# Eight weight pieces of the next group split during the output's passes, and x's eight tiles ahead of the context's eight

## The chip, the cores and the metric

The kernel runs on one core of one Trainium2 chip. The metric is the device time of the whole program in microseconds (us), and the median of several runs is what counts. The core has five engines, each with an instruction queue of its own: TensorE (PE in the rows; PEld is its weight load), VectorE (DVE), ScalarE (ACT), GpSimd (POOL) and SyncE (SP), which here only issues DMAs. They meet at semaphores. An instruction that waits holds up all that stands behind it on its own engine.

## What is computed

Two layers of a transformer over 256 latent tokens ("x") and 256 context tokens, 1024 channels wide. Each layer has a mixer block (four kinds of attention from one projection `w_in`, gated and merged, then `w_out`) and a SwiGLU block (`w_ffn_in`, `w_ffn_out`). Around both stands a sandwich of RMS norms:

```python
def rmsnorm(x, g):
    xf = x.astype(jnp.float32)
    y = xf * lax.rsqrt(jnp.mean(xf * xf, axis=-1, keepdims=True) + EPS)
    return (y * g.astype(jnp.float32)).astype(x.dtype)

def gated_merge(gate_pre, branches, w_branch, w_out):
    o = jnp.stack(branches, axis=2)
    up = jnp.einsum('btnw,nwd->btnd', o, w_branch)
    g = jax.nn.sigmoid(gate_pre.reshape(up.shape))
    return jnp.sum(g * up, axis=2) @ w_out

def swiglu(u, w1, w2):
    a, b = jnp.split(u @ w1, 2, axis=-1)
    return (jax.nn.silu(a) * b) @ w2
```

What matters here is the seam between two blocks. The block's output y (tokens by 1024) is normed and added to the residual stream H, H is normed again into u, u is scaled and shifted by the conditioning, and the next block begins with u times its first weight matrix. The last layer's context tokens are not needed after its keys and values, so there the second half works on the 256 latent tokens alone.

## The kernel before

**Numbers.** All is float32, made of two fp32r parts: a high part (rounded by ScalarE) and a low part (the rest, by VectorE or GpSimd). A product is three matmuls: high by high, low by high, high by low.

**Weights.** A weight piece is 128 rows by up to 512 columns. SyncE loads it into one of four places of `load_ring` (256 KB, as two DMAs of 128 KB where its columns come from two places). A step `split` then makes its parts: ScalarE's copy makes the high part (line 1538), and then VectorE (1738) or GpSimd (1493) makes the low part, into one of the five places of `w_ring`. The load of piece i may begin when the low part of piece i-4 is made. `build_plan` writes all steps into one list in order; each engine runs its own steps in that order. At its end (1046 to 1060) a loop puts the splits in: before a step of piece n all pieces up to n+3 are split, as far as the place of `w_ring` has been given back (`piece_used`).

**The output** (`output`, 895) writes y in two halves of 512 channels. For each half it takes 8 pieces (mixer) or 22 (SwiGLU), and each piece serves all four token tiles (128 tokens each; two in the last layer's case). The last five pieces of the second half are different: `passes(tt, ...)` runs all five for token tile 0, then for tile 1, and so on, so that tile 0 is done early. So all five places of `w_ring` stay taken until the last tile's passes. While passes run, the norms of the tiles already done are made: sum of squares of y (`ysq`, ScalarE, 1555), y times the gain (`yg`, VectorE, 1820), its root (GpSimd, 1460), new H (`hn`, 1841), sum of squares of H (`hsq`, ScalarE, 1562), root, and u = H times root in two halves (`un_a`, `un_b`, VectorE, 1859).

**The next group** (`begin`, 339) is the first product of the next block: eight pieces ("first 0" to "first 7"), each of which feeds four PSUM banks at once. For each of the eight tiles of 128 channels, TensorE transposes u (`ut`, 2127), ScalarE scales and shifts it and makes the high part (`apA`, 1594 and 1599), VectorE makes the low part (`apB`, 1865), and then come the matmuls (2150 with the high part of u, 2155 with its low part). x's tokens are tiles 0 and 1, the context's are 2 and 3. The order is: x with pieces 0 to 4, the context with pieces 0 to 4 (256 columns each), then pieces 5 to 7 with all 512 columns. `hooks` puts norm steps of token tiles 2 and 3 between these. Transposed tiles go through three banks in turn (`turned_by`, 300).

There are three such seams: **seam 1**, layer 0's mixer output to its SwiGLU (about 750 to 803 us in the trace); **seam 2**, layer 0's SwiGLU output to layer 1's mixer (about 1143 to 1189 us); **seam 3**, layer 1's mixer output to its SwiGLU, x alone (about 1637 to 1671 us). At seam 3 a step `warm` runs 26 matmuls whose results are not used while the norms end.

## Time and profile before

| | us |
|---|---|
| median of 3 runs | 1860.78 |
| the three runs | 1861.15, 1853.61, 1860.78 |
| the profiled execution | 1853.27 |
| its span, first to last instruction | 1851.3 |
| TensorE busy | 1756.7 (95%) |
| VectorE, ScalarE, GpSimd busy | 1152.2, 875.3, 585.9 |
| mean granted TensorE clock | 0.983 of full |

The profiled execution lies at the lower of the three runs, and two of the three are some 7.5 us longer. A time in the rows is one of that execution, counted from the span's start. Busy time of TensorE is no measure of its speed, as its matmuls overlap: a matmul of 512 columns is shown with 390 ns, and the next begins 227 ns after it. So lengths are taken here from start to start.

### The profile page before, as it was taken

Reading aid. Unit: us, or ns where it says so; the run is one execution under the profiler, and the core shown is the slowest. Engines: PE = TensorE matmul, PEld = TensorE weight load, DVE = VectorE, ACT = ScalarE, POOL = GpSimd, SP = SyncE. Lnnn points to the kernel's source line nnn. Section 1 sums busy time; section 2 is a strip of 40 time slices with the busy share of each in tenths; the row PEclk is TensorE's granted clock in tenths of the full one; section 3 lists DMA queues with packets and bytes.
Section 4 is the critical chain, followed back from the end, with each engine's and each line's share of the span. In section 5 each row is a group of like instructions: output and inputs, shape, how many; then the busy total and the mean of one; then the engine's idle time right before and its main releaser. Section 6 shows DMA issues by size and latency. Waiting matters only on the chain. (4 is left out here: it accounts for less than half of the span.)

```text
span 1851.3 us, 30506 instructions
## 1 busy us (share of the span) xinstructions
PE 1756.7 (95%) x10166; PEld 1489.5 (80%) x10166; DVE 1152.2 (62%) x2348; ACT 875.3 (47%) x1906; POOL 585.9 (32%) x555
## 2 busy tenths in 40 slices
PE   7999999999999999899999999888999999999998
PEld 3777888778788787788888888777898788979997
DVE  4256578687676765567777663555564456765655
ACT  5566555444344443552222222666565455565543
POOL 0344434455455452111111000224335654321100
PEclk8999999999999999999999999999999999999999
DMA  7222233344433325245556663233343333446665
GB/s 299 58 66 66 69 92 90 91 123 124 110 94 96 80 63 166 90 120 148 148 150 209 219 202 69 71 90 88 88 124 98 92 76 85 121 148 176 183 200 159
DMA packets 341253, 224.14 MB, mean 121 GB/s; under 512 B 57654, under 2 KB 322156, under 8 KB 340076
## 3 DMA queue, kind: packets, MB, share of 16 engines
q1 hardware_dynamic: 331692, 215.88, 41.2%
q10 hardware_dynamic: 9408, 6.32, 1.3%
q8 instruction: 84, 1.38, 0.3%
q14 instruction: 69, 0.57, 0.1%
HBM read 221.06 MB, written 1.07 MB: 120 GB/s over the span
## 5 line engine op out<-in xcount | busy, mean ns | idle before, releaser
L1996 PE MATMUL bank<-Uhi,w_ring 128*128 128x512 f32 (+1 forms) x1536 | 547.4, 356 | 19.0 <-ACT H L1673 7.5
L1998 PE MATMUL bank<-Uhi,w_ring 128*128 128x512 f32 (+1 forms) x1536 | 531.5, 346 | 0.0
L1997 PE MATMUL bank<-Ulo,w_ring 128*128 128x512 f32 (+1 forms) x1536 | 531.3, 346 | 0.0
L1538 ACT ACTIVATE w_ring<-load_ring 128x512 fp32r<-128x512 f32 (+3 forms) x632 | 369.8, 607 | 148.3 <-PE bank L1998 105.1
L1738 DVE TENSOR_TENSOR w_ring<-load_ring,w_ring 128x512 fp32r<-128x512 f32 (+1 forms) x424 | 319.1, 768 | 179.1 <-ACT w_ring L1538 154.9
L1996 PEld LDWEIGHTS bank<-Uhi,w_ring 128*128 128x128 f32 x1536 | 294.3, 192 | 60.3 <-ACT H L1673 10.5
L1493 POOL TENSOR_TENSOR w_ring<-load_ring,w_ring 128x512 fp32r<-128x512 f32 (+3 forms) x208 | 246.4, 1190 | 251.7 <-ACT w_ring L1538 136.2
L1998 PEld LDWEIGHTS bank<-Uhi,w_ring 128*128 128x128 f32 x1536 | 294.2, 192 | 36.4
L1997 PEld LDWEIGHTS bank<-Ulo,w_ring 128*128 128x128 f32 x1536 | 294.9, 192 | 30.1
L1481 POOL TENSOR_TENSOR Y<-Y,small 128x512 f32<-128x512 f32 x160 | 173.3, 1083 | 289.8 <-DVE small L1942 276.9
L1947 DVE TENSOR_TENSOR Z<-bank,Z 128x512 fp32r<-128x512 f32 x160 | 109.7, 686 | 96.5 <-ACT Z L1659 94.1
L1651 ACT ACTIVATE Y<-bank,small 128x512 f32<-128x512 f32 (+1 forms) x192 | 117.0, 611 | 91.4 <-DVE small L1925 91.2
L1510 POOL TENSOR_TENSOR Z<-fil,Z 128x512 fp32r<-128x512 f32 (+1 forms) x44 | 44.6, 1016 | 319.4 <-ACT Z L1691 319.4
L1996 PE MATMUL bank<-w_ring,Z 128*128 128x512 f32 x360 | 141.9, 394 | 2.4 <-DVE fil L1964 1.1
L1998 PE MATMUL bank<-w_ring,Z 128*128 128x512 f32 x360 | 140.3, 390 | 0.0
L1997 PE MATMUL bank<-w_ring,Z 128*128 128x512 f32 x360 | 140.2, 389 | 0.0
L1659 ACT ACTIVATE Z<-bank 128x512 fp32r<-128x512 f32 x160 | 95.3, 595 | 68.7 <-PE bank L2243 66.9
L1759 DVE SCALAR_TENSOR_TENSOR mod_sums<-mod_place,sc,mod_sums 128x256 f32<-128x256 f32 x224 | 124.8, 597 | 3.1
L1996 PE MATMUL bank<-Z 128*64 128x256 f32 (+2 forms) x368 | 111.4, 303 | 12.4 <-DVE Z L1947 10.2
L1996 PE MATMUL bank<-Z,w_ring 128*128 128x512 f32 (+3 forms) x304 | 107.7, 354 | 6.4 <-DVE Z L1891 4.9
L1918 DVE TENSOR_REDUCE small<-bank 128x1 f32<-128x512 f32 x160 | 108.8, 680 | 3.0 <-PE bank L1998 2.9
L1998 PE MATMUL bank<-Z 128*64 128x256 f32 (+2 forms) x368 | 106.6, 290 | 0.0
(141 smaller groups left out, 2651.3 us busy)
## 6 DMA issues: line engine op xcount, KB each, us to landing
load_ring<-in_w_in SPq DMA_DIRECT2D x192, 256.0 KB, 2.9
load_ring<-in_w_ffn_in SPq DMA_DIRECT2D x160, 256.0 KB, 3.1
mod_ring<-in_w_mod SPq DMA_DIRECT2D x96, 256.0 KB, 3.3
load_ring<-in_w_ffn_out SPq DMA_DIRECT2D x88, 256.0 KB, 3.2
mod_place<-in_w_mod SPq DMA_DIRECT2D x64, 256.0 KB, 2.8
load_ring<-in_w_branch SPq DMA_DIRECT2D x64, 256.0 KB, 2.9
mod_w<-in_w_mod SPq DMA_DIRECT2D x8, 1024.0 KB, 15.8
load_ring<-in_w_in SPq DMA_DIRECT2D x64, 128.0 KB, 2.5
```

Of the source, the lines that this page charges most:

```text
L1481: pool.tensor_tensor(prob('Pn', key).rearrange("p (m k) -> p m k", m=m), prob('P', key).rearrange("p (m k) -> p m k", m=m), small[:, plan. ...
L1493: pool.tensor_tensor(w_ring[:, slot, 1, 0:sz], load_ring[:, plan.slot['load', key], 0:sz], w_ring[:, slot, 0, 0:sz].bitcast(F32), ALU.subt ...
L1538: act.activation(w_ring[:, plan.slot['w', key], 0, 0:sz], load_ring[:, plan.slot['load', key], 0:sz], ACT.Copy).then_inc(sem['w_hi'], 1)
L1651: ins = act.activation(prob('P', key)[:, a:b], s_bank(key)[:, a:b], ACT.Exp, bias=sm[:, 2 + i:3 + i], scale=scale_of(key), accum_out=sm[:, ...
L1659: act.activation(dst, src, ACT.Copy).then_inc(sem['pt_hi'], 1)
L1738: dve.tensor_tensor(w_ring[:, slot, 1, 0:sz], load_ring[:, plan.slot['load', key], 0:sz], w_ring[:, slot, 0, 0:sz].bitcast(F32), ALU.subtr ...
L1759: ins = dve.scalar_tensor_tensor(out=a, in0=w, scalar=by, in1=a, op0=ALU.mult, op1=ALU.add)
L1918: dve.tensor_reduce(sm[:, 0:m], s_bank(key)[:, :].rearrange("p (m k) -> p m k", m=m), AX_X, ALU.max).then_inc(sem['max_ready'], 1)
L1947: dve.tensor_tensor(dst, src, hi.bitcast(F32), ALU.subtract).then_inc(sem['pt_lo'], 1)
L1996: pe.matmul(dst, lhs[0], rhs[0], start=start, stop=False)
L1997: pe.matmul(dst, lhs[0], rhs[1], start=False, stop=False)
L1998: return pe.matmul(dst, lhs[1], rhs[0], start=False, stop=stop)
```

## The change

The group's eight pieces no longer go through `w_ring`. `w_place` gives each a place of its own in the big buffer Z, where the attention's outputs (seams 1 and 3) or the hidden values of the first channels (seam 2) have been used up once the piece before the passes is done (`w_free`). A new step `early` names the points at which they are split: pieces 0 to 3 between the first tile's passes, 4 and 5 after its new H, 6 and 7 in the group itself. In the group, x goes through all eight pieces first, and then the context goes through all eight, 256 columns each time. Two of x's tiles, 3 and 5, are scaled by VectorE instead of ScalarE (`apC`). Some norm steps move by one place.

```diff
+SCALED_BY_DVE = ((0, 3), (0, 5))
...
-        ring = ('b3', 'pv', 'b4')[p.turns % 3]
-        p.turns += 1
+        ring = ('b3', 'b4', 'pv')[(side * KT + kt) % 3]
...
+        parts = [('gmm_a' if both else 'gmm', 0, kt) for kt in range(KT)] + [('gmm_b', 1, kt) for kt in range(KT * both)]
...
-            passes(0, 0, W_RING)
+            if nxt:
+                p.early[nxt] = ('piece_used', (key, early - 1))
+            for kt in range(W_RING):
+                passes(0, kt, kt + 1)
+                if nxt and kt < 4:
+                    early_split(nxt, kt + 1)
             y_sum(nmo, 1, 0)
             y_scale(nmo, 0)
             h_both(nmo, 0)
+            if nxt:
+                early_split(nxt, 6)
...
-                return {'last': [lambda turn_first: turn_first()]}
+                return {'last': [lambda turn_first: turn_first()], 2: [lambda: early_split(nxt, KT)]}
...
-                    0: [lambda: h_new(nmo, 2, 0), lambda: y_sum(nmo, 1, 3), lambda: h_new(nmo, 2, 1)],
-                    1: [lambda: y_scale(nmo, 3), lambda: h_sums(nmo, 2), lambda: h_stat(nmo, 2)],
-                    2: [lambda: h_both(nmo, 3), lambda: u_next(nmo, 2)],
-                    3: [lambda: h_sums(nmo, 3), lambda: h_stat(nmo, 3)],
-                    4: [lambda: u_next(nmo, 3)]}
+                    0: [lambda: h_new(nmo, 2, 1)],
+                    1: [lambda: y_sum(nmo, 1, 3), lambda: y_scale(nmo, 3)],
+                    2: [lambda: h_sums(nmo, 2), lambda: h_stat(nmo, 2), lambda: h_both(nmo, 3), lambda: early_split(nxt, 7)],
+                    3: [lambda: u_next(nmo, 2)],
+                    4: [lambda: h_sums(nmo, 3), lambda: h_stat(nmo, 3), lambda: early_split(nxt, KT)],
+                    5: [lambda: u_next(nmo, 3)]}
...
+        if st[0] == 'early':
+            while done < len(use) and (use[done][0] != st[1] or use[done][1] < st[2]['upto']) and (
+                    use[done][0] in p.early or ringed[place[use[done]] - W_RING] in used):
+                done = split()
+            continue
```

Three places of the queues, before and after. In these rows line numbers shift: 1538, 1555, 1562, 1738, 1841, 1859 and 1865 before are 1574, 1591, 1598, 1776, 1879, 1897 and 1912 after. A split whose target is Z is one of the group's pieces; one whose target is `w_ring` is any other.

Place 1, ScalarE during the passes of seam 1, before: after the five last splits of the output come the first two tiles' sums.

```order
L1538 ACTIVATE w_ring<-load_ring 128x512 x5
L1555 ACTIVATE tmp,y_sums<-bank 128x512 x2
L1562 ACTIVATE tmp,h_sums<-H 128x512 x4
L1538 ACTIVATE w_ring<-load_ring 128x512
L1555 ACTIVATE tmp,y_sums<-bank 128x512
```

The same place after:

```order
L1574 ACTIVATE w_ring<-load_ring 128x512 x5
L1574 ACTIVATE Z<-load_ring 128x512 x4
L1591 ACTIVATE tmp,y_sums<-bank 128x512
L1574 ACTIVATE Z<-load_ring 128x512 x2
L1591 ACTIVATE tmp,y_sums<-bank 128x512
L1598 ACTIVATE tmp,h_sums<-H 128x512 x4
```

Four splits now stand ahead of the first tile's sum of squares, and two more ahead of the second's.

Place 2, VectorE in the group of seam 1, around the norm of token tile 3, before (the row of L1859 is tile 3's u):

```order
L1865 TENSOR_TENSOR Ulo<-fil,Uhi 128x256
L1846 TENSOR_SCALAR row_stat<-h_sums 128x1
L1852 SCALAR_TENSOR_TENSOR row_stat<-h_sums,row_stat 128x1
L1865 TENSOR_TENSOR Ulo<-fil,Uhi 128x256
L1859 TENSOR_SCALAR Y<-H,row_stat 128x512 x2
L1865 TENSOR_TENSOR Ulo<-fil,Uhi 128x256 x4
L1738 TENSOR_TENSOR w_ring<-load_ring,w_ring 128x512
```

The same place after:

```order
L1912 TENSOR_TENSOR Ulo<-fil,Uhi 128x256
L1884 TENSOR_SCALAR row_stat<-h_sums 128x1
L1890 SCALAR_TENSOR_TENSOR row_stat<-h_sums,row_stat 128x1
L1776 TENSOR_TENSOR w_ring<-load_ring,w_ring 128x512 x5
L1912 TENSOR_TENSOR Ulo<-fil,Uhi 128x256
L1897 TENSOR_SCALAR Y<-H,row_stat 128x512 x2
L1912 TENSOR_TENSOR Ulo<-fil,Uhi 128x256 x10
```

Five low parts of later pieces (ordinary pieces of the SwiGLU block) now stand between tile 3's root and its u; the low part of x's sixth tile is behind them too. Seam 2 has the same rows with five pieces of the gates.

Place 3, VectorE in the group of seam 3, before, from the low parts of x's first three tiles on:

```order
L1865 TENSOR_TENSOR Ulo<-fil,Uhi 128x256 x3
L1738 TENSOR_TENSOR w_ring<-load_ring,w_ring 128x512
L1865 TENSOR_TENSOR Ulo<-fil,Uhi 128x256 x2
L1738 TENSOR_TENSOR w_ring<-load_ring,w_ring 128x512
L1865 TENSOR_TENSOR Ulo<-fil,Uhi 128x256 x2
L1738 TENSOR_TENSOR w_ring<-load_ring,w_ring 128x512
L1865 TENSOR_TENSOR Ulo<-fil,Uhi 128x256
L1738 TENSOR_TENSOR w_ring<-load_ring,w_ring 128x512 x4
```

The same place after:

```order
L1912 TENSOR_TENSOR Ulo<-fil,Uhi 128x256 x3
L1776 TENSOR_TENSOR Z<-load_ring,Z 128x512
L1776 TENSOR_TENSOR w_ring<-load_ring,w_ring 128x512 x5
L1912 TENSOR_TENSOR Ulo<-fil,Uhi 128x256 x5
L2026 TENSOR_TENSOR tmp<-tmp,bank 128x256 x2
```

Six low parts of weights stand in a row between x's third and fourth tile.

## Rows read from the trace of the kernel before

**Rows 1.** The page, part 1: busy us (share of the span) and instructions.

```profile
PE 1756.7 (95%) x10166; PEld 1489.5 (80%) x10166; DVE 1152.2 (62%) x2348; ACT 875.3 (47%) x1906; POOL 585.9 (32%) x555
```

**Rows 2.** Waits of TensorE, whole span: us in total, times, longest.

```profile
PE bank L2127 <- DVE Y L1859: 11.3, 6, 2.5
PE bank L2127 <- DVE Y L1820: 2.1, 1, 2.1
```

**Rows 3.** TensorE in order of time, seam 1: start, us, work [idle before, releaser].

```profile
777.46 0.30 PE L2127 MATMUL bank<-C,Y 128*128 128x128 f32 x1 [1.86 <-DVE Y L1859]
780.22 0.48 PE L2127 MATMUL bank<-C,Y 128*128 128x128 f32 x1 [2.46 <-DVE Y L1859]
780.35 2.06 PE L2150 MATMUL bank<-Uhi,w_ring 128*128 128x256 f32 x8
...
785.76 1.19 PE L2150 MATMUL bank<-Uhi,w_ring 128*128 128x256 f32 x8
...
792.80 1.19 PE L2150 MATMUL bank<-Uhi,w_ring 128*128 128x256 f32 x8
...
794.30 0.60 PE L2127 MATMUL bank<-C,Y 128*128 128x128 f32 x4
...
797.49 1.98 PE L2150 MATMUL bank<-Uhi,w_ring 128*128 128x512 f32 x8
...
800.21 1.98 PE L2150 MATMUL bank<-Uhi,w_ring 128*128 128x512 f32 x8
```

**Rows 4.** Stretches of seam 1: length, busy by engine, clock, DMA share, GB/s.

```profile
780.35:785.20 4.85, 4.85 (x24) 4.85 (x25) 0.99 (x3) 1.96 (x4) 0.00 (x0) 0.51 0.12 38
785.76:787.40 1.64, 1.64 (x17) 1.64 (x16) 0.23 (x1) 0.98 (x2) 0.00 (x0) 1.00 0.04 10
```

**Rows 5.** ScalarE, VectorE and SyncE in order of time, passes of seam 1.

```profile
757.49 0.60 ACT L1555 ACTIVATE tmp<-bank 128x512 f32<-128x512 f32 x1 [2.71 <-PE bank L1998]
...
754.87 0.69 DVE L1738 TENSOR_TENSOR w_ring<-load_ring,w_ring 128x512 fp32r<-128x512 f32 x1 [1.75 <-ACT w_ring L1538]
...
755.59 0.80 SPq L1430 DMA_DIRECT2D load_ring<-in_w_ffn_in  x2
```

**Rows 6.** VectorE and GpSimd in order of time, group of seam 1.

```profile
771.42 1.40 DVE L1841 SCALAR_TENSOR_TENSOR H<-Y,row_stat,H 128x512 f32<-128x512 f32 x2
...
774.49 2.43 DVE L1841 SCALAR_TENSOR_TENSOR H<-Y,row_stat,H 128x512 f32<-128x512 f32 x2
...
774.94 1.43 POOL L1493 TENSOR_TENSOR w_ring<-load_ring,w_ring 128x512 fp32r<-128x512 f32 x1
```

**Rows 7.** VectorE, SyncE and ScalarE in order of time, end of seam 3.

```profile
1664.16 0.69 DVE L1738 TENSOR_TENSOR w_ring<-load_ring,w_ring 128x512 fp32r<-128x512 f32 x1 [1.80 <-ACT w_ring L1538]
...
1664.88 1.59 SPq L1430 DMA_DIRECT2D load_ring<-in_w_ffn_in  x2
...
1667.78 1.38 ACT L1538 ACTIVATE w_ring<-load_ring 128x512 fp32r<-128x512 f32 x2 [2.30 <-DMA load_ring<-in_w_ffn_in]
```

**Rows 8.** ScalarE in order of time: tile 3's second sum, and seam 3's scaling.

```profile
777.18 0.62 ACT L1562 ACTIVATE tmp<-H 128x512 f32<-128x512 f32 x1
...
1656.60 0.42 ACT L1599 ACTIVATE Uhi<-fil 128x256 fp32r<-128x256 f32 x1
```

**Rows 9.** TensorE in order of time, seam 3.

```profile
1658.87 1.20 PE L2150 MATMUL bank<-Uhi,w_ring 128*128 128x256 f32 x8
1659.90 0.65 PE L2155 MATMUL bank<-Ulo,w_ring 128*128 128x256 f32 x4
...
1671.36 0.39 PE L1996 MATMUL bank<-Uhi,w_ring 128*128 128x256 f32 x1 [1.76 <-DVE tmp L1979]
```

**Rows 10.** TensorE in order of time, seam 2.

```profile
1158.04 0.44 PE L2127 MATMUL bank<-C,Y 128*128 128x128 f32 x2 [2.07 <-DVE Y L1820]
...
1175.03 0.71 PE L2150 MATMUL bank<-Uhi,w_ring 128*128 128x256 f32 x4
...
1175.96 0.72 PE L2150 MATMUL bank<-Uhi,w_ring 128*128 128x256 f32 x4
```

More of the change, by code:

```diff
@@ L353, in turn_in @@
                 side, kt = tiles[i]
-                turn(nm, side, kt, range(NTOK // P) if whole[i] else range(2 * side, 2 * side + 2))
+                turn(nm, side, kt, range(2 * side, 2 * side + 2))
         def scale(i):
@@ L1044, in build_plan, with split @@
         p.take('load', key, (p.lo[key], key))
-        p.take('w', key, ('piece_used', key))
+        if key[0] not in p.early:
+            p.take('w', key, ('piece_used', key))
     order, done, begun, used = [], 0, set(), set()
-    for st in S:
-        piece = st[0] in ('mm', 'mm_a', 'gmm', 'gmm_a', 'gmm_b', 'ym', 'ym_a', 'ym_b')
+    ringed = [key for key in use if key[0] not in p.early]
+    place = {key: i for i, key in enumerate(ringed)}
+    def split():
+        order.append(('split', use[done], {'raises': (p.lo[use[done]],)}))
+        return done + 1
+    for st in S:
+        piece = st[0] in ('mm', 'mm_a', 'mm_b', 'gmm', 'gmm_a', 'gmm_b', 'ym', 'ym_a', 'ym_b')
+        if st[0] == 'early':
[3 more added lines that the diff above has]
+            continue
         if piece or st[0] == 'mod0row':
@@ L1051, in build_plan @@
             while done < min(len(use), first + AHEAD) and (
-                    done <= first or done < W_RING or use[done - W_RING] in used):
-                order.append(('split', use[done], {'raises': (p.lo[use[done]],)}))
-                done += 1
+                    done <= first or use[done][0] not in p.early and (
+                        place[use[done]] < W_RING or ringed[place[use[done]] - W_RING] in used)):
+                done = split()
             if piece:
@@ L1587, in _ @@
                         act.wait_ge(sem['u_turned'], count['u_turned', key])
[L1588 to L1589 removed]
+                        parts = [(side, 0, ut_bank(f['bank'])[:, 0:f['cols']])]
                     else:
```

87 lines of the change are left out of this document (52 added, 35 removed).

## The prediction

> **What bounds the kernel now.** I read the page first: TensorE is busy for 1756.7 of 1851.3 us [rows 1], so a gain can only come from its 95 us of idle time or from a slow clock, and a loss comes at once where TensorE is made to wait. Then the table of its waits: the longest are the transposes of u waiting for VectorE, 11.3 and 2.1 us [rows 2], and all of them lie at the three seams. Then TensorE in order of time there. At seam 1 the context's first transpose waits 1.86 us for token tile 2's u and 2.46 us for tile 3's [rows 3], and in the 4.85 us behind that the granted clock is 0.51, its 1.2 GHz level, then 1.00 again [rows 4]. The two pieces run there took 785.76 - 780.35 = 5.41 us [rows 3], where one takes 1.64 [rows 4], so the slow clock cost 2.1 us. Seam 2 repeats this. It also has a wait of 2.07 us before x's first tile [rows 10]. At seam 3 the group runs without a break, and TensorE waits 1.76 us only behind it [rows 9].
>
> So the change aims at something real: 1.86 + 2.46 + 2.1 = 6.4 us at each of seams 1 and 2. What I have to find is what comes late next.
>
> **Part 1: x's eight tiles first.** The context's first transpose moves behind three more pieces of x, 3 x 1.64 = 4.9 us of cover for tiles 2 and 3. Taken alone, the 4.3 us of waiting and the slow clock go: -6.4 us at seams 1 and 2, nothing at seam 3, which has no context. The price: pieces 5 to 7 run twice with 256 columns instead of once with 512. A 256-column piece without its turn takes 794.30 - 792.80 = 1.50 us and a 512-column one 800.21 - 797.49 = 2.72 [rows 3], so +0.28 for each, +0.8 us at seam 1. At seam 2 the context uses only two of the four banks and its half of a piece costs 0.93 with its turn [rows 10]. I take +0.6 there.
>
> **Part 2: the splits during the passes.** They cost TensorE nothing themselves, but they stand ahead of the norm chain on ScalarE. Piece 3 of the group needs the load place of the output's last piece, whose low part ends at 755.56. SyncE issues the two DMAs from 755.59 to 756.39 [rows 5]. A load took 1667.78 - 1664.88 = 2.9 us from issue to the split that waited for it [rows 7]. Half as large, I take 2.2 from the second issue, so piece 3's high part runs at about 758.3 to 758.9. The first tile's sum of squares, at 757.49 now [rows 5], stands behind it: 1.4 us late. One shared step later, tile 1's u is about 1.2 us late, and x's first transpose with it.
>
> To that comes GpSimd. Two of VectorE's H updates took 2.43 us while GpSimd's split ran beside them, against 1.40 without [rows 6]: +1.0. The change puts pieces 1, 3 and 5 on GpSimd just when the first tiles' y and H are made, so I count one such collision for each seam, +1.0 us.
>
> The Trainium skill (SBUF — State Buffer, Who interferes with whom) says that a VectorE instruction with two inputs in SBUF is blocked for as long as a GpSimd instruction that reads SBUF holds the shared port, and one with a single SBUF input is not. By that rule the H update (both inputs in SBUF) is hit and the product of a PSUM bank with the gain is not, which is why I count one collision and not two; [rows 6] show the first, and no row here the second. By a rule that both collide, each seam would lose 0.7 us more.
>
> At seam 1 a part of this is given back, as VectorE's split ahead of x's first low part goes. I take +1.0 for seam 1, +1.1 for seam 2, where the 2.07 us wait loses its present cause (the bank that y's tile 2 holds) and gets this one, and +1.0 for seam 3.
>
> **Part 3: five more splits in a burst.** This decides. The loop for an `early` step stops at its limit only for pieces of the named group. Once piece 7 is split the next piece is another's, the test is true, and it goes on for as long as `w_ring` has room. It has: all five places. So the queues get piece 7 and then five ordinary pieces in a row (place 2; at seam 3 pieces 6 and 7 and five more, place 3). Behind them on VectorE wait tile 3's u and the low part of x's sixth tile, on ScalarE x's seventh tile; for these waits TensorE.
>
> Their data is not there yet. Only four load places exist, so the fourth of the five may be loaded only after piece 7's low part is made, the fifth only after the first's. From T, when ScalarE takes up piece 7: its high part 0.6, GpSimd's low part 1.4 [rows 6] (it waits for tile 3's root first, some 0.2), load 2.9 [rows 7], ScalarE's last two high parts 1.4 [rows 7], VectorE's low part 0.7 [rows 7], and the low part of x's tile 0.4 (as ScalarE's of equal size [rows 8]). T + 7.6 us, or T + 7.1 if GpSimd is free at once.
>
> Seam 1: T follows tile 3's second sum on ScalarE. It ends at 777.8 now [rows 8]. In the new order two of ScalarE's roundings wait for VectorE's scaling, and tile 3's H waits on VectorE for tile 2's sums. Following both queues with the durations above I get T near 781.6. TensorE runs x's pieces 0 to 4 and the high part of piece 5 meanwhile, and waits there some 1.9 us itself for two low parts that stand behind those H updates. It would stop at 781.9 and go on at 789.1: **a wait of 7.2 us**. If T stays at 777.8, TensorE stops near 779.9 and waits 5.5. I take 7.2, since the longer queue is in the order itself, and keep 5.5 for the range. A wait of 4.3 us brought the slow clock [rows 3, 4], so this one does too: +2.1, zero at the least.
>
> Seam 2 has the same steps; the loads are whole DMAs of 208 or 256 KB: the same 7.2 + 1.9 + 2.1.
>
> Seam 3: T is the end of the scaling of x's fourth tile, 1657.0 [rows 8]. Here piece 6 is in the burst as well, and the last split's load waits behind two others: its low part ends near 1664.3 and x's fourth low part near 1664.7. TensorE comes to that low part at 1659.90 [rows 9]: **4.8 us**, and 2.1 for the clock. In return the next pieces are all split, and the 1.76 us wait behind the group [rows 9] goes.
>
> **Sum.** Seam 1: -6.4 + 0.8 + 1.0 + 1.9 + 7.2 + 2.1 = +6.6. Seam 2: -6.4 + 0.6 + 1.1 + 1.9 + 7.2 + 2.1 = +6.5. Seam 3: +1.0 + 4.8 + 2.1 - 1.8 = +6.1. Together **+19 us**, 1.0%. Against the profiled execution that is 1853.3 + 19 = 1872; against the median, 1860.8 + 19 = 1880. The three runs lie at either level, so I take the middle, **1876**. A measurement of this kernel can tell about 0.5% (9 us) from no change.
>
> **Rivals.**
>
> A, *the burst costs queue time only*: the loads are there when ScalarE comes to them (as for the first three of the five, whose loads can begin earlier). Then the release is T + 0.6 + 5 x 0.5 + 0.7 + 0.4, about T + 4.3, some 3 us earlier at each seam: +19 - 9 = +10, 1863 to 1871; and without a fall of the clock at any seam +4. For it: the splits in the passes come early, so the ring is ahead. Against it: the rule of four load places, and [rows 7], where ScalarE stands 2.30 us for just such a load. Chance 0.14.
>
> B, *the cover holds*, the other side: tile 3's u is ready before TensorE ends x's pieces, because the five extra splits either come ahead of T or don't hold VectorE. Place: VectorE's low part of x's sixth tile. Then seam 1 keeps -6.4 + 0.8 + 1.0 + 1.9 = -2.7, seam 2 -2.8 and seam 3 -0.8: -6 us, and -12 if the low parts are not late either (1.9 twice, 1.0 or so twice). 1841 to 1855. It decides where the burst's wait falls under 2.7 us with the clock kept, so if that low part were done by 784.6 and not 789. Chance 0.13.
>
> C, *worse*: TensorE's slow stretches grow longer than 5 us, or the loads, behind the four conditioning loads that SyncE takes up at seam 1 in the same stretch, land late: +30 or more. Chance 0.05. The forecast, +11 to +29, has 0.68.
>
> **Range and chances.** The low ends of the terms (5.5 and no slow clock at seams 1 and 2, no collision) lead to about +9, and A without the clock's fall to +4: 1857. The high end is +29 on the upper level: 1890. So 1856 to 1890, which leaves out most of B and C. Faster by over 0.5%: 0.10, the better half of B. Within 0.5%: 0.18. Slower: 0.72.
>
> **What would show it.** In the changed profile: TensorE's wait for u's tiles 2 and 3 gone; in its place one of 5 to 7 us at seams 1 and 2 before a matmul with the low part of u (line 2202 of the new code), released by VectorE, and one of 4 to 5 at seam 3; ahead of it ScalarE's split waiting some 3 us for a load, twice in a burst; a granted clock near 0.5 behind each; the first sum of squares over 1 us later after the first passes; no wait of 1.76 us behind seam 3's group. The forecast is wrong if the five splits run without a wait for a load, or if TensorE has work from x's tiles until they are done.

## The result, and the profile after

The changed kernel takes **1888.6 us** (median of 4 runs, 1887.6 to 1888.8) against 1858.8 us of the kernel before beside it (4 runs, 1853.6 to 1861.2): 1.0163 times as long, 95% interval 1.0144 to 1.0183, a loss of 29.9 us. The prediction said 1876, 1856 to 1890, and slower. The profiled executions have spans of 1887.0 and 1851.3 us, so in the rows 35.7 us are to be accounted for: the profiled execution of the kernel before was the fastest of its runs, and beside the experiments below its median was 1853.6 to 1856.3 us, not 1858.8. So where versions measured at different times are compared, differences of medians can be off by some 5 us, and the ratio to the kernel before beside each is the safer number.

First the page of the changed kernel, part 1, then TensorE's two longest waits. They answer to [rows 1] and [rows 2].

```profile
PE 1762.5 (93%) x10220; PEld 1497.8 (79%) x10220; DVE 1158.5 (61%) x2358; ACT 875.9 (46%) x1908; POOL 585.7 (31%) x555
```

```profile
PE bank L2174 <- DVE Y L1897: 23.5, 6, 15.5
PE bank L2202 <- DVE Ulo L1912: 21.7, 5, 7.3
```

TensorE's busy time grew by only 6 us. The rest is waiting. Waits for a low part of u (line 2202) took 1.5 us of the kernel before and take 21.7 now. Waits for u itself (line 2174) doubled, from 11.3 to 23.5, and one of them alone is 15.5 us.

To place the difference I use four rows of TensorE that every kernel here has, with nearly the same wait, and the end of the span. These are the rows of before:

```profile
725.20 0.50 PE L1996 MATMUL bank<-w_ring,Z 128*128 128x512 f32 x1 [0.54 <-DVE fil L1964]
1033.47 0.50 PE L1996 MATMUL bank<-w_ring,Z 128*128 128x512 f32 x1 [0.26 <-DVE fil L1986]
1222.46 0.58 PE L1996 MATMUL bank<-Uhi,w_ring 128*128 128x256 f32 x1 [3.04 <-ACT under L1673]
1291.62 0.79 PE L1996 MATMUL bank<-Uhi,w_ring 128*128 128x512 f32 x1 [3.34 <-DVE Z L1891]
```

(In no_burst the third row's wait is 2.94 us, in all others 3.02 to 3.04.) The first stretch between them holds seam 1, the second seam 2, the third the start of layer 1's attention, the last the remaining attention and seam 3. Each number below is the difference of two such rows of one trace, in us:

| kernel | seam 1 | seam 2 | attention's start | rest, seam 3 | span |
|---|---|---|---|---|---|
| before | 308.3 | 189.0 | 69.2 | 559.7 | 1851.3 |
| after | 315.6 | 209.3 | 69.4 | 567.4 | 1887.0 |
| no_burst | 306.5 | 200.4 | 69.4 | 562.8 | 1863.9 |
| put_late | 313.5 | 198.6 | 69.4 | 569.8 | 1876.9 |
| both | 306.1 | 190.3 | 70.1 | 559.1 | 1851.5 |
| before_put_late | 308.7 | 203.0 | 69.2 | 558.3 | 1864.2 |
| old_order | 307.9 | 198.7 | 69.4 | 560.0 | 1861.8 |
| burst_3 | 308.4 | 196.0 | 69.4 | 563.6 | 1862.7 |
| put_attn | 306.3 | 185.3 | 71.9 | 563.4 | 1854.2 |
| tuned | 306.4 | 185.2 | 71.6 | 561.0 | 1849.7 |
| x_by_act | 305.6 | 185.1 | 73.4 | 563.7 | 1853.5 |
| best | 304.6 | 186.0 | 69.7 | 573.1 | 1859.2 |
| before_put_quiet | 307.5 | 188.0 | 69.2 | 574.6 | 1865.5 |
| final | 305.6 | 185.0 | 69.6 | 560.1 | 1846.5 |

So the loss is 7.3 us at seam 1, 20.3 at seam 2 and 7.7 in the last stretch. Of the last one some 4 us can be chance: no_burst and both have the same order behind the fourth row, and differ by 3.7 there.

**Seam 1** went as forecast. TensorE of the changed kernel in order of time, then ScalarE and VectorE, and the stretches around the wait (length, busy, clock, DMA share, GB/s):

```profile
768.06 0.33 PE L2174 MATMUL bank<-C,Y 128*128 128x128 f32 x1 [0.93 <-DVE Y L1897]
769.86 0.47 PE L2174 MATMUL bank<-C,Y 128*128 128x128 f32 x1 [1.47 <-DVE Y L1897]
...
780.24 0.74 PE L2202 MATMUL bank<-Ulo,Z 128*128 128x256 f32 x4 [1.57 <-DVE Ulo L1912]
...
791.07 1.23 PE L2202 MATMUL bank<-Ulo,Z 128*128 128x256 f32 x4 [7.28 <-DVE Ulo L1912]
```

```profile
783.01 0.62 ACT L1574 ACTIVATE Z<-load_ring 128x512 fp32r<-128x512 f32 x1
783.53 1.66 ACT L1574 ACTIVATE w_ring<-load_ring 128x512 fp32r<-128x512 f32 x3
788.52 1.39 ACT L1574 ACTIVATE w_ring<-load_ring 128x512 fp32r<-128x512 f32 x2 [3.33 <-DMA load_ring<-in_w_ffn_in]
```

```profile
784.24 2.75 DVE L1776 TENSOR_TENSOR w_ring<-load_ring,w_ring 128x512 fp32r<-128x512 f32 x3 [0.86 <-ACT w_ring L1574]
789.24 1.45 DVE L1776 TENSOR_TENSOR w_ring<-load_ring,w_ring 128x512 fp32r<-128x512 f32 x2 [2.24 <-DMA load_ring<-in_w_ffn_in]
790.60 0.42 DVE L1912 TENSOR_TENSOR Ulo<-fil,Uhi 128x256 fp32r<-128x256 f32 x1
```

```profile
785.00:790.00 5.00, 0.00 (x0) 0.67 0.67 192
790.00:795.00 5.00, 3.93 (x18) 0.50 0.46 127
795.00:800.00 5.00, 5.00 (x37) 0.81 0.00 0
```

The reader sees the burst: piece 7's high part at 783.01, three further pieces at once, 3.33 us of waiting for a load, two more pieces; VectorE follows, and x's sixth low part, which TensorE wants since 783.79, comes at 790.60. The waits for u's tiles 2 and 3 of [rows 3] (1.86 and 2.46 us) are gone, as forecast, and a wait of 7.28 us stands in their place, with the slow clock behind it. (That wait is itself cover for tile 3's u; no_burst shows what is left without it.)

**Seam 2** has the same wait (7.02 us) and one that the prediction does not have. TensorE, then ScalarE and SyncE:

```profile
1178.87 0.45 PE L2174 MATMUL bank<-C,Y 128*128 128x128 f32 x1 [15.46 <-DVE Y L1897]
...
1201.63 1.22 PE L2202 MATMUL bank<-Ulo,Z 128*128 128x256 f32 x4 [7.02 <-DVE Ulo L1912]
```

```profile
1146.76 1.01 ACTq L1604 DMA_DIRECT2D gain_kept<-coef  x2
...
1169.19 1.06 ACT L1574 ACTIVATE Z<-load_ring 128x416 fp32r<-128x416 f32 x2 [17.09 <-DMA load_ring<-in_w_in]
1170.16 0.58 ACT L1591 ACTIVATE tmp<-bank 128x512 f32<-128x512 f32 x1
```

```profile
1152.03 10.12 SPq L1469 DMA_DIRECT2D load_ring<-in_w_in  x3
```

ScalarE stands 17.09 us for the load of a piece of the group, and behind that split stands the first tile's sum of squares (1170.16). So all of the norm chain is late, and TensorE waits 15.46 us for x's first tile. The loads are slow. The DMA part of the page for 1146 to 1170 says what else is on the queues (packets, bytes, share; then median us from issue to landing):

```profile
q1 hardware_dynamic: 613, 0.92, 51.9%
q10 hardware_dynamic: 2080, 0.01, 4.9%
...
load_ring<-in_w_in SPq DMA_DIRECT2D x5, 208.0 KB, 17.6
```

2080 packets that carry 0.01 MB are the write of layer 1's two gains into DRAM, value by value. The loads beside them take 17.6 us instead of 2.5 to 3. The kernel before has the same write, at 1139.31, and its load issued at 1144.59 was slow too:

```profile
load_ring<-in_w_in SPq DMA_DIRECT2D x1, 208.0 KB, 15.1
```

It landed at 1159.7, and ScalarE split that piece only at 1163.57, without a wait.

**Seam 3** has the burst's wait, 5.12 us (forecast 4.8), and the 1.76 us wait of [rows 9] is gone:

```profile
1680.24 0.30 PE L2174 MATMUL bank<-C,Y 128*128 128x128 f32 x1 [2.97 <-DVE Y L1897]
...
1696.79 1.22 PE L2202 MATMUL bank<-Ulo,Z 128*128 128x256 f32 x4 [5.12 <-DVE Ulo L1912]
```

### The profile page after: what moved, and what is told of

Same layout as the page of the kernel before. It is cut to its first block and busy times, and to the rows that moved or that the text cites. A ratio compares the mean times of both kernels' runs of the same rounds, so it can differ in the third digit from the quotient of the medians.

```text
span 1887.0 us, 30638 instructions
## 1 busy us (share of the span) xinstructions
PE 1762.5 (93%) x10220; PEld 1497.8 (79%) x10220; DVE 1158.5 (61%) x2358; ACT 875.9 (46%) x1908; POOL 585.7 (31%) x555
## 5 line engine op out<-in xcount | busy, mean ns | idle before, releaser
L1574 ACT ACTIVATE w_ring<-load_ring 128x512 fp32r<-128x512 f32 (+3 forms) x608 | 355.6, 608 | 153.8 <-PE bank L2045 104.4
L1776 DVE TENSOR_TENSOR w_ring<-load_ring,w_ring 128x512 fp32r<-128x512 f32 (+1 forms) x412 | 310.4, 770 | 167.3 <-ACT w_ring L1574 140.2
L1530 POOL TENSOR_TENSOR w_ring<-load_ring,w_ring 128x512 fp32r<-128x512 f32 (+3 forms) x196 | 231.8, 1189 | 215.5 <-ACT w_ring L1574 119.3
```

The costliest lines, as they stand in the source:

```text
L1530: pool.tensor_tensor(w_place(key, 1)[:, 0:sz], load_ring[:, plan.slot['load', key], 0:sz], w_place(key, 0)[:, 0:sz].bitcast(F32), ALU.subt ...
L1574: act.activation(w_place(key, 0)[:, 0:sz], load_ring[:, plan.slot['load', key], 0:sz], ACT.Copy).then_inc(sem['w_hi'], 1)
L1776: dve.tensor_tensor(w_place(key, 1)[:, 0:sz], load_ring[:, plan.slot['load', key], 0:sz], w_place(key, 0)[:, 0:sz].bitcast(F32), ALU.subtr ...
```

## Experiments

Two theories for the loss: the burst of five splits behind the group's last piece (Part 3), and the gain write that holds up the loads. Each is undone alone, then both.

**no_burst**

```diff
+    ends = {key[0]: i + 1 for i, key in enumerate(use)}
...
-            while done < len(use) and (use[done][0] != st[1] or use[done][1] < st[2]['upto']) and (
+            while done < ends[st[1]] and (use[done][0] != st[1] or use[done][1] < st[2]['upto']) and (
```

> The changed kernel with one edit: a step for early splits ends with the last piece of the group that it names, so the five pieces behind it are split at their ordinary times, four pieces ahead of their use. Everything else stays. Theory (the burst holds VectorE and ScalarE, as in Part 3): the three waits before a matmul with the low part of u, 7.28, 7.02 and 5.12 us, go, and with them some of the slow clock behind each (2.1 us at each at most), 19 to 25 us together: 1864 to 1870 against 1888.6. The gain write's delay at seam 2 stays (15.46 us). Rival 1 (tile 3's own chain is late anyway, the burst only stands beside it): the wait shrinks by less than half at seams 1 and 2, 1877 or more. Rival 2 (the pieces behind the group are late without the burst): the waits go, but new ones of several us show at the first piece behind each group, 1875 or more.

Measured: 1865.2 us, 1.0060 of before (1.0045 to 1.0075), 23.4 less than the changed kernel by the medians, 19 by the ratios, 23.1 by the spans. The three waits are gone from the table of waits (low parts of u: 2.7 us in all, two waits), and no new wait comes with the first piece behind the group. Seam 1 is 1.8 us **shorter** than before now. The first theory holds: the burst cost 19 us of waiting and the slow clock behind it. Two things differ from what I expected. The write's wait at seam 2 did not stay at 15.46 us but is 12.78 here. And the wait for tile 3's u is not all hidden: in this order it is still 1.08 us at seam 1 (0.87 at seam 2), which the burst's own wait had covered. The same row in both:

```profile
785.37 0.33 PE L2175 MATMUL bank<-C,Y 128*128 128x128 f32 x1 [1.08 <-DVE Y L1898]
```

**put_late**

```diff
             begin(nm, l, 0, first, NTOK // P, follow)
+            for g in range(2):
+                p.step('rowput', (l, g), sides=1)
...
-                for g in range(2):
-                    p.step('rowput', (l + 1, g), sides=1)
```

> The changed kernel with one edit: the two writes of layer 1's gains into DRAM (each 1024 values of 4 bytes by one DMA of ScalarE's queue) are issued behind the first group of layer 1 instead of ahead of the last output passes of layer 0. They are read only at layer 1's outputs. Theory (these small packets hold up the loads of the group's pieces, and the piece's split stands ahead of the first sum of squares on ScalarE): the load that took 17.1 us too long lands in under 4, the 15.46 us wait at seam 2 goes, and seam 2 looks as seam 1: 13 to 17 us less, 1872 to 1876 against 1888.6. Rival (the load is slow for another reason, such as its own DRAM rows or the loads of the conditioning weights ahead of it): no change, 1887 to 1890, with the same wait on the load.

Measured: 1876.4 us, 1.0122 (1.0107 to 1.0137), 12.2 less than the changed kernel by the medians, 8 by the ratios, 10.1 by the spans. The 15.46 us wait is gone, and ScalarE waits under 2 us for the loads there:

```profile
1152.74 0.55 ACT L1574 ACTIVATE Z<-load_ring 128x416 fp32r<-128x416 f32 x1 [1.95 <-DMA load_ring<-in_w_in]
```

The second theory holds too, but the gain is short of 13 to 17. Behind the group, where the write now stands, a new wait of 5.12 us comes at 1215.50. The next two runs show more of it.

**both** (the two edits together)

> The changed kernel with both edits: early splits end with their group, and the two gain writes are issued behind layer 1's first group. Theory (two separate causes, both on TensorE's path): the gains add up, 19 to 25 and 13 to 17, so 1847 to 1857 against 1888.6, and 0.995 to 1.000 of the kernel before; what is left are the waits for two low parts at each seam and the later norm chain (Part 1's gain of 6.4 less Part 2's price). Rival (one hides behind the other at seam 2): there only the longer of the two comes back, 7 us less than the sum, about 1860.

Measured: 1855.9 us, 1.0013 (1.0004 to 1.0022). The causes add up within the noise: by the medians 23.4 and 12.2 are 35.6, and 32.7 came back; by the spans 23.1 and 10.1 are 33.2, and 35.5 came back. The write's new place has a price of its own, which put_late pays too. Behind the group, TensorE's waits for a bank are longer than in before (0.78 and 0.47 there), and the clock is slow behind them:

```profile
1193.69 0.58 PE L2044 MATMUL bank<-Uhi,w_ring 128*128 128x256 f32 x1 [3.05 <-ACT under L1714]
1200.09 0.55 PE L2044 MATMUL bank<-Uhi,w_ring 128*128 128x256 f32 x1 [1.93 <-ACT under L1714]
```

**before_put_late** (the kernel before with the same move of the write)

> The kernel before with the two gain writes issued behind layer 1's first group, nothing else. In its trace the same load also landed 15.1 us after its issue, but its piece was needed only later, and TensorE waited 2.07 us before x's first tile. Theory (the slow load was there and hidden): the load lands in under 4 us, and the time moves by 0 to -3 us. Rival (the slow loads cost the kernel before as well, through the pieces that come later): more than 5 us faster.

Measured: 1864.8 us, 1.0052 (1.0035 to 1.0070): 11 us **slower**. My expectation was wrong in its sign. The load at the old place did get fast, and that was worth nothing, since it had been hidden; at the new place the write met loads that were wanted soon:

```profile
1184.88 0.38 ACTq L1568 DMA_DIRECT2D gain_kept<-coef  x1
...
1206.53 0.63 ACT L1538 ACTIVATE w_ring<-load_ring 128x512 fp32r<-128x512 f32 x1 [10.68 <-DMA load_ring<-in_w_in]
```

```profile
1207.49 0.58 PE L1996 MATMUL bank<-Uhi,w_ring 128*128 128x256 f32 x1 [11.57 <-ACT under L1673]
```

So a write's price goes with what the loads behind it lack in slack. Whether a place without a price exists was the open question of the next runs.

**put_attn** (no burst; the two writes inside layer 1's attention)

```diff
                 owed = run_slot(k, micros[k], owed + quota[k - a])
+                if l and k in (5, 7):
+                    p.step('rowput', (l, k // 7), sides=1)
...
-                for g in range(2):
-                    p.step('rowput', (l + 1, g), sides=1)
...
+    ends = {key[0]: i + 1 for i, key in enumerate(use)}
...
```

> The changed kernel with early splits ending with their group (as in both), and layer 1's two gain writes issued inside layer 1's attention, one behind each of two slots of it, where the loads are four pieces ahead of their use. In both, the writes stand behind layer 1's first group, and TensorE waits 3.05 and 1.93 us there for a bank that ScalarE empties (0.78 and 0.47 in the kernel before), with a slow clock from 1193.7 to 1203.4. Theory (the writes hold loads up wherever they stand, and it costs what the loads have no slack for): these two waits shrink to under 1 us each and the clock stays up, 4 to 8 us less than both: 1848 to 1852, and below the kernel before (1853.6). Rival 1 (the waits there belong to the new split order): no change against both, 1854 to 1858. Rival 2 (the writes hold up attention's loads as well): slower than both, 1860 or more.

Measured: 1857.4 us, 1.0010 (0.9995 to 1.0025). The two waits shrank to 0.78 and 0.47 us as the theory says, and seam 2's stretch is 5.1 us shorter than in both. But attention's start is 1.7 us longer (a wait of 1.62 us for a low part appears at 1261.54, another grew from 1.56 to 2.40), and the rest 4.3 longer. Of these, only the 1.7 us have waits to show for them; the rest is within what can be chance there. So rival 2 holds in part: the writes moved a part of their price. Against no_burst, which has the writes at their old place, seam 2 is 15.1 us shorter (200.4 to 185.3): that is the write's whole price there.

**tuned** (put_attn, and pieces 3 to 5 split later)

```diff
-                if nxt and kt < 4:
+                if nxt and kt < 3:
                     early_split(nxt, kt + 1)
             y_sum(nmo, 1, 0)
+            if nxt:
+                early_split(nxt, 4)
             y_scale(nmo, 0)
             h_both(nmo, 0)
-            if nxt:
-                early_split(nxt, 6)
...
             u_next(nmo, 1)
+            early_split(nxt, 6)
```

> As put_attn, and of the group's pieces only the first three are split ahead of the first tile's sum of squares; piece 3 is split behind that sum, pieces 4 and 5 behind the second tile's u. This undoes the part of Part 2 that stands ahead of the norm chain (in both, piece 3's split starts at 758.88 and the first sum of squares at 759.42; the kernel before has it at 757.49). Theory (the early splits delay the chain by what they stand for in ScalarE's queue): the first sum of squares comes 1.9 us earlier, and TensorE's waits for u of the first two tiles (0.30 and 1.47 at seam 1, 0.39 and 1.41 at seam 2, 3.17 and 1.41 at seam 3) shrink by 1 to 1.8 us at each seam: 3 to 5 us less than put_attn. Rival (the chain's length from the first tile's sum is bound by VectorE and GpSimd, or the moved splits come late for pieces 4 and 5): within 1 us of put_attn, or slower by 1 to 4 us.

Measured: 1855.5 us, 1.0005 (0.9990 to 1.0019), 2 us less than put_attn with overlapping intervals. ScalarE, first of both, then of tuned:

```profile
758.88 0.63 ACT L1575 ACTIVATE Z<-load_ring 128x512 fp32r<-128x512 f32 x1 [1.84 <-DMA load_ring<-in_w_ffn_in]
759.42 0.58 ACT L1592 ACTIVATE tmp<-bank 128x512 f32<-128x512 f32 x1
```

```profile
757.87 0.60 ACT L1594 ACTIVATE tmp<-bank 128x512 f32<-128x512 f32 x1 [1.14 <-PE bank L2048]
```

The sum of squares is 1.55 us earlier (1.25 counted from the row at 725), so Part 2's mechanism is shown. But seams 1 and 2 are no shorter (306.4 and 185.2 against 306.3 and 185.3): VectorE makes piece 4's low part between u's second tile and y's third, and x's second transpose now waits 1.38 us at seam 1 and 1.08 at seam 2 for that y. The edit also brings a collision of its own. It puts piece 5's split on GpSimd just when VectorE makes u's second tile, which takes 1.91 us instead of the 0.88 of put_attn (1.71 at seam 2). VectorE, then GpSimd:

```profile
767.67 1.91 DVE L1900 TENSOR_SCALAR Y<-H,row_stat 128x512 f32<-128x512 f32 x2 [0.66 <-POOL row_stat L1502]
```

```profile
767.99 1.31 POOL L1533 TENSOR_TENSOR Z<-load_ring,Z 128x512 fp32r<-128x512 f32 x1 [0.35 <-issue]
```

So the rival holds for the splits as they were moved. It is not shown that the delay of the first sum is worth nothing: best, below, has it undone without this collision.

**burst_3** (both, with a burst of three pieces behind the group's last one; the edit against both)

```diff
-            while done < ends[st[1]] and (
+            while done < ends[st[1]] + 3 * (st[2]['upto'] == KT) and (
```

> As both, but behind the group's last piece three further pieces are split in a row (the changed kernel splits five, both none). The first three have their loads in time; only the fourth and fifth wait for a load place. Theory (7 us is 3.3 us of waiting for loads and the rest time in the queues): TensorE's wait before x's sixth low part comes back at about half, 3 to 4 us at seams 1 and 2 and 1 to 2.5 at seam 3, with some slow clock behind it: 7 to 14 us more than both, 1863 to 1870. Rival A (only the waits for loads cost; without them the queues keep up): within 2 us of both, 1855 to 1858. Rival B (any splits there hold the queues for the full 7 us): 1872 or more.

Measured: 1866.5 us, 1.0071 (1.0048 to 1.0094), 10.6 more than both. TensorE, seam 1, then ScalarE of the same place:

```profile
779.24 1.22 PE L2203 MATMUL bank<-Ulo,Z 128*128 128x256 f32 x4 [1.99 <-DVE Ulo L1913]
786.41 0.74 PE L2203 MATMUL bank<-Ulo,Z 128*128 128x256 f32 x4 [2.09 <-DVE Ulo L1913]
```

```profile
782.54 1.66 ACT L1575 ACTIVATE w_ring<-load_ring 128x512 fp32r<-128x512 f32 x3
```

Without a wait for a load, the burst costs TensorE 2.1 us where five pieces cost 7.3. That is less than the 3 to 4 I expected. By stretches the three pieces cost seam 1 2.3 us against both, where the five of the changed kernel cost 9.5; the other 7.2 are the wait for loads (3.33 us of it on ScalarE), the last two splits and the slow clock, which no run separates. The total of 10.6 is not all the burst's. Seam 2 is 5.7 longer, though the burst's wait there is 1.87 us: the gain write behind the group now costs waits of 2.35 and 4.88 us. The last stretch is 4.5 longer, with a wait of 1.67 us at seam 3.

**x_by_act** (put_attn with `SCALED_BY_DVE = ()`: ScalarE scales all of x)

> As put_attn, but all tiles of x are scaled by ScalarE as in the kernel before (the changed kernel has VectorE scale x's tiles 3 and 5, and ScalarE only round them). Theory (Part 3's 1.9 us: the low parts of x's tiles 3 and 5 are late because their scaling stands in VectorE's queue behind the H updates of tiles 2 and 3): the waits before a matmul with the low part of u, 1.22 at seam 1 and 1.90 at seam 2, go, and the time falls by 2 to 3 us against put_attn. Rival (the low part itself stands behind the H updates, so it is late whoever scales): the waits stay within 0.5 us and ScalarE's extra work delays tile 3's sums: 0 to 3 us more than put_attn.

Measured: 1855.0 us, 0.9994 (0.9977 to 1.0010), 2.3 less than put_attn with overlapping intervals. The waits for a low part shrank from 1.47 to 0.77 us at seam 1 and from 1.89 to 1.13 at seam 2, and did not go. So VectorE's scaling is about 0.7 us of each; the rest is the low part's own place behind the H updates.

**old_order** (both, but five tiles of x, then five of the context, then whole tiles, with ScalarE's scaling and the places of the norm steps, as before)

```diff
-        parts = [('gmm_a' if both else 'gmm', 0, kt) for kt in range(KT)] + [('gmm_b', 1, kt) for kt in range(KT * both)]
+        parts = [('gmm_a', 0, kt) for kt in range(W_RING)] + [('gmm_b', 1, kt) for kt in range(W_RING)] if both else \
+            [('gmm', 0, kt) for kt in range(W_RING)]
+        parts += [('gmm', 0, kt) for kt in range(W_RING, KT)]
...
```

> As both (early splits end with their group, writes behind layer 1's first group), but x's first five tiles are followed by the context's first five and then whole tiles, as in the kernel before, and ScalarE scales all of them. So only the places of their own and the splits during the passes are left of the change. It prices Part 1. Theory (the order hides the context's u): the waits for u of tiles 2 and 3 come back at seams 1 and 2, 1.9 and 2.5 us or more, with a slow clock of 2.1 us behind; against that the 1.2 and 1.9 us waits for a low part go and 0.6 to 0.8 us for halved pieces: 3 to 6 us more at each seam, 6 to 12 us more than both, 1862 to 1868. Rival (places of their own alone would do, since the pieces are there earlier): within 3 us of both.

Measured: 1868.1 us, 1.0067 (1.0054 to 1.0080), 12.2 more than both (10 by the ratios). The number is at the end of the range, and most of it is not for my reason. The waits for tiles 2 and 3 did come back (1.08 and 2.46 us at seam 1, 1.13 and 2.36 at seam 2), but seam 1 is only 1.8 us longer than in both. At seam 2, 8.4 us longer, there is one wait of 9.10 us behind the group, where the write stands, and one of 3.04 before x's first tile.

That seam 1 is only 1.8 longer has a cause in the trace of both: a slow clock at x's first pieces, which old_order and the kernel before do not have. The stretch from 770 to 773 us in both, then in old_order:

```profile
770.00:773.00 3.00, 3.00 (x13) 2.59 (x13) 2.34 (x6) 2.11 (x5) 0.55 (x1) 0.51 0.00 0
```

```profile
770.00:773.00 3.00, 3.00 (x23) 2.39 (x21) 2.51 (x7) 2.72 (x7) 0.55 (x1) 1.00 0.00 0
```

From x's second transpose to its first matmul with a low part of u it takes 3.73 us in both and 2.55 in old_order, 1.2 us for the clock. The changed kernel, put_attn, x_by_act and final have this slow stretch too, no_burst does not; what decides it no run shows, as the waits of 0.3 and 1.5 us ahead of it are alike in both and old_order.

**best** (put_attn's idea, with the writes at slots 20 and 26; ScalarE scales; pieces 4 and 5 split behind the scaling of y's third tile)

```diff
-SCALED_BY_DVE = ((0, 3), (0, 5))
+SCALED_BY_DVE = ()
...
             y_scale(nmo, 2)
+            early_split(nxt, 6)
...
+                if l and k in (20, 26):
+                    p.step('rowput', (l, k // 26), sides=1)
```

> The three findings together, on top of the changed kernel: early splits end with their group; pieces 3 to 5 are split behind the first sum of squares and behind the scaling of y's third tile (tuned had pieces 4 and 5 just ahead of it, where x's first low parts and the product of y's third tile waited 1.38 and 1.08 us for VectorE); all of x is scaled by ScalarE; and layer 1's two gain writes are issued behind slots 20 and 26 of layer 1's attention, where TensorE was busy for 60.0 of 60 us (1350 to 1410) and the other queues have slack, instead of slots 5 and 7 (which cost 1.62 and 0.8 us there). Theory (each takes its own waits away): 2.4 us for the writes, 1.5 for ScalarE's scaling, 2 to 4 for the splits, against put_attn: 1846 to 1852, 0.995 to 0.998 of the kernel before. Rival (what is taken away at one wait comes back at the next, since VectorE's queue is full over the seam): 1853 to 1857, no difference from before.

Measured: 1860.4 us, 1.0029 (1.0019 to 1.0038). Seam 1 is the shortest of all (304.6, 1.0 us under x_by_act), but one write stood at the wrong place. I had chosen it by TensorE's busy time. ScalarE, then TensorE:

```profile
1373.93 0.38 ACTq L1607 DMA_DIRECT2D gain_kept<-coef  x1
...
1386.76 0.63 ACT L1577 ACTIVATE w_ring<-load_ring 128x512 fp32r<-128x512 f32 x1 [8.71 <-DMA load_ring<-in_w_in]
```

```profile
1387.71 0.58 PE L2046 MATMUL bank<-Uhi,w_ring 128*128 128x256 f32 x1 [7.96 <-ACT merge_sum L1716]
```

**before_put_quiet** (the kernel before, the writes at slots 20 and 26)

> The kernel before with layer 1's two gain writes at slots 20 and 26 of layer 1's attention, nothing else. It shows what of best's gain is the writes' place and not the change. Theory: in the kernel before the writes are hidden but for the 2.07 us wait before x's first tile at seam 2, whose released bank hangs on y's tile and not on a load, so 0 to -2 us; with the writes behind the first group it was 11 us slower by one 11.57 us wait. Rival (the writes cost wherever they stand): 1 to 5 us slower.

Measured: 1867.8 us, 1.0070 (1.0057 to 1.0083), 13 us slower, with the same wait, 8.16 us at 1393.14. The rival holds, and more strongly than written. That TensorE is busy says nothing about the loads' slack.

**final** (x_by_act, with the writes placed by the loads' slack: one ahead of the stretch of seam 2 in which SyncE issues few loads and none is wanted for 12 us, one at slot 7)

```diff
             passes(1, 0, W_RING if nts > 2 else 1)
             y_sum(nmo, 1, 1)
+            if which == 1:
+                p.step('rowput', (l + 1, 0), sides=1)
...
+                if l and k == 7:
+                    p.step('rowput', (l, 1), sides=1)
```

> As x_by_act (early splits end with their group, ScalarE scales all of x), but the first of layer 1's two gain writes is issued on ScalarE's queue in the output's second passes of layer 0, just ahead of the first tile's sums of H, and the second behind slot 7 of layer 1's attention. A write held loads up for some 13 us wherever it stood. Behind the first one stand only the loads of pieces 6 and 7 and of the next pieces, which are wanted some 12 us later (piece 6's split was at 1162.33 in x_by_act, the write would be at 1148.2). Theory (the price of a write is what the loads in the 13 us behind it lack in slack): the first costs nothing there, the second 0.8 us as in put_attn, so 1.6 us less than x_by_act, 0.996 to 0.999 of the kernel before. Rival (the shadow is longer or the loads of pieces 6 and 7 are late by it): a wait of 2 us or more for a low part or for x's tile in seam 2, and 1.001 or more.

Measured: **1849.0 us**, 0.9975 (0.9963 to 0.9987). It is the only version here that beats the kernel before beyond its interval, and it is 1.8% below the changed kernel by the two ratios. The write goes out at 1148.13. It held loads here too: piece 7's, issued at 1147.1, landed after 10.7 us, and the two issued behind the write after 9.3. But piece 7 is split only at 1167.46 and the next ones from 1169.70 on; in seam 2 TensorE's longest wait is 1.41 us:

```profile
1148.13 0.38 ACTq L1607 DMA_DIRECT2D gain_kept<-coef  x1
```

```profile
1156.19 0.33 PE L2177 MATMUL bank<-C,Y 128*128 128x128 f32 x1 [1.41 <-DVE Y L1900]
1165.28 0.74 PE L2205 MATMUL bank<-Ulo,Z 128*128 128x256 f32 x4 [1.11 <-DVE Ulo L1915]
```

Seams 1 and 2 are 2.7 and 4.0 us shorter than before (308.3 to 305.6, 189.0 to 185.0), the two stretches behind are 0.4 us longer each, and the one ahead of the first row 0.9. So the change's aim was sound; what it is worth without its burst, with ScalarE's scaling and the writes out of the way, is 4.8 us of span, 5.7 of median.

## Why the prediction was right, and where it was not

**Part 1** was right in direction, and too large. It took the whole wait and the slow clock as gone, 6.4 us, less 0.8 for halved pieces. Between old_order and both seam 1 differs by 1.8 us. The traces show where the rest went. The cover of three pieces is too short: in both TensorE still waits 1.08 us for tile 3's u. A low part comes 1.22 us late (forecast 1.9). The slow clock at x's first pieces costs 1.2 us; no term of the sum has it. And old_order's first wait is 1.08 us, not 1.86. In the changed kernel the first of these did not show, because the burst's wait covered it.

**Part 2**: piece 3's split ran at 758.45 (forecast 758.3 to 758.9) and the first sum of squares at 758.99, 1.5 us late (forecast 1.4). The collision is there as well: two H updates took 2.46 us beside GpSimd's split, as in [rows 6]. At seam 1 it comes out at 0.7 us (forecast 1.0): the waits at x's first two tiles are 0.93 and 1.47 us, where the kernel before had 0.65 and 1.02. How much could be had by taking this delay away is open: tuned gained nothing at seams 1 and 2 but put a new collision in its place, and best, without that one, has seam 1 1.0 us shorter than x_by_act and seam 2 0.9 longer.

**Part 3** was right in mechanism, place and size. T was 783.0 (forecast 781.6), the release T + 8.0 (forecast T + 7.6), the wait 7.28, 7.02 and 5.12 us (forecast 7.2, 7.2, 4.8). no_burst took all three away. Two numbers in its working were off. The load of 2.9 us [rows 7] was counted from the issue at 1664.88, but the load that the split at 1667.78 waited for had been issued at 1663.88 and took 3.9 us to land; in the burst of seam 1 it was 3.3 us from the end of piece 7's low part (785.25) to the split at 788.52, which is most of the 0.4 us between T + 8.0 and T + 7.6. And with GpSimd free at once its own terms give T + 7.4, not T + 7.1. Rival A, queue time only, is refuted by the 3.33 us wait for a load and by burst_3. Rival B is what no_burst shows: seam 1 is then 1.8 us under before, where B said 2.7.

**The sum.** Seam 1: forecast +6.6, measured +7.3, of it 9.1 us for the burst (forecast 7.2 + 2.1) and -1.8 for all the rest (forecast -2.7). Last stretch: forecast +6.1 for seam 3, measured +7.7 with some 4 us of chance. (Seam 3 was read as running without a break before; its trace has waits of 2.17 and 0.84 us at the first tiles, 2.97, 1.41 and 0.42 after.) Seam 2: forecast +6.5, measured +20.3.

The step that failed is the sentence "Seam 2 has the same steps". It has one more, the gain write on ScalarE's queue just ahead of the passes. I had costed the moved splits at a load of 2.2 to 2.9 us from seams 1 and 3 and never asked how long a load takes at seam 2's own time. The row was there to read: before's load issued at 1144.59, beside the write, took 15.1 us. It cost nothing then because its piece was wanted late, and **the change took that cover away**. The stretches of seam 2 close the account: without burst and write (put_attn) it is 185.3 us, 3.7 under before (forecast -2.8); the write adds 15.1 (no_burst), and the burst 8.9 (the changed kernel; forecast 9.3). So two of the three terms were right, and the third, 15.1 us, was put at nothing. In all, put_late got 12.2 us back and not 15.1, as its write stands at a place with a price of its own. Rival C foresaw loads that land late, but named another cause (the conditioning loads of seam 1) and gave it 0.05.

That the total came out inside the range is luck in part. Its high end was 14 us above the forecast, and no term stands for that end, least of all one for seam 2's load. Against the profiled executions alone the forecast was +19 us and the measured loss 35.7.

## What to carry to other kernels

A loop that works ahead "as far as there is room" must end with the group that it serves; behind the group, each piece it takes stands in front of the chain's next step, and the ones whose load is not there stop the queue. Before a consumer is moved earlier, read how long its load takes at that time and place, not at a like place. The write of many small packets had no fixed price in this kernel: one held the loads issued near it until 10 to 13 us later, two until 22 us, and the price was what those loads lacked in slack. So put such a transfer where the next pieces are wanted last, and look for that on the load queue, not on the busiest engine.

## What the runs showed of the hardware

**A 4 KB write slowed the loads around it.** One write of 1024 values of 4 bytes (1040 packets) went out at 1373.93 in best; the load that ScalarE waited for came at 1386.76, 12.8 us later. From 1380 to 1384 the DMA engines were 46 to 52% busy and moved 21 to 27 GB/s; at 1386 to 1388, 326 GB/s. Two writes in a row held loads for 21.7 us in before_put_late (1184.88 to 1206.53) and 22.4 in the changed kernel (1146.76 to 1169.19). Even SyncE's issue got longer: three issues took 10.12 us at 1152.03, two of them 5.2 and 4.4 us, where two took 0.80 in [rows 5]. The Trainium skill (DMA: Bandwidth & Descriptors, Specifications) says that transfers below 512 B make the DMA engine read, modify and write, and (Queues, rings and completion order) that an engine takes turns between the queues it has work for, packet by packet; by that, the loads would share turns with the small packets. The rows agree only in that both queues are at work in the same stretch. They don't show the turns as the cause: from 1146 to 1170 in the changed kernel the 2080 small packets hold the engines for 4.9%, and the 613 packets of the loads for 51.9%, which is 0.32 us a packet, against 0.06 in put_late, from 1140 to 1162, where no write stands (2352 packets, 38.8%). So the loads' own packets took longer, and why stays open.

**GpSimd and VectorE.** In both at seam 1, the two instructions that make u's tile 3 took 1.88 us beside GpSimd's split, against 0.87 for tile 2 without one, though each has a single tile as input. And the product of a PSUM bank with the gains kept its 0.69 us beside a split that ran from 763.08 to 764.81. VectorE, then GpSimd:

```profile
763.57 0.69 DVE L1859 TENSOR_TENSOR Y<-bank,gain_rows 128x512 f32<-128x512 f32 x1
...
779.77 0.87 DVE L1898 TENSOR_SCALAR Y<-H,row_stat 128x512 f32<-128x512 f32 x2
...
783.83 1.88 DVE L1898 TENSOR_SCALAR Y<-H,row_stat 128x512 f32<-128x512 f32 x2 [0.44 <-POOL row_stat L1500]
```

```profile
763.08 1.73 POOL L1531 TENSOR_TENSOR Z<-load_ring,Z 128x512 fp32r<-128x512 f32 x1 [1.49 <-DMA load_ring<-in_w_ffn_in]
...
783.76 1.27 POOL L1531 TENSOR_TENSOR Z<-load_ring,Z 128x512 fp32r<-128x512 f32 x1
```

The product row bears out the rule that the prediction cited and had no row for. The prediction left out the rule's condition, and the u rows fall under it. The Trainium skill (SBUF — State Buffer, Who interferes with whom) says that an instruction with one SBUF input does collide where it runs in a mode that uses both port pairs, and that `tensor_scalar` can. The u rows agree in their lengths, here and in tuned; the mode itself no row shows. The prediction's sum did not suffer: in the changed kernel the pairs that make u took 0.87 to 0.88 us at seam 1, since the burst keeps tile 3's u until GpSimd is done. In both the pair of tile 3 is 1.0 us longer by it.
